# A three-part fused block on one core: the level copies of the gated recurrence go to ScalarE, the state-space scan runs in pairs of steps, and the output's second half is transposed after the first chunk

## The reference

```python
# first block: modulation vectors from a conditioning vector, 6 * D wide for each of two layers
m = jax.nn.silu(cond) @ w_mod + b_mod
# hybrid mixer, gated delta rule in chunks: a unit lower triangular system per chunk and head
lower = where(strict, einsum("nbhcd,nbhsd->nbhcs", kb, kc) * decay, 0)
sol = triangular_solve(lower + eye, rhs, left_side=True, lower=True, unit_diagonal=True)
def step(state, xs_i):                       # 4 steps in each of two directions, in this kernel
    v_new = u_i - einsum("bhcd,bhde->bhce", w_i, state)
    new_state = state * exp(gl_i) + einsum("bhcd,bhce->bhde", kt_i, v_new)
    o_i = einsum(qd_i, state) + einsum(a_i, v_new)
y_lat = concatenate([delta_readout(o_lat_a, za_l, n_tok), o_lat_b], -1) @ w_out   # o_lat_b: softmax attention

# second block: state-space mixer, 32 groups of 16 channels with 64 complex states each
bu = einsum('gph,blgh->blgp', b_bar, uf)     # complex
states = associative_scan(a_bar * s + bu)    # over the 256 tokens
y = einsum('ghp,blgp->blgh', c_re, real(states)) - einsum(..., c_im, imag(states)) + d_skip * uf
y = gelu(y); y = y * sigmoid(einsum('blgh,ghk->blgk', y, w_glu))
```

## Time and profile before

| | us |
|---|---|
| median of 3 runs | 1442.45 |
| the profiled execution | 1443.34 |
| its span | 1441.4 |
| PE busy | 1338.2 (93%) |
| DVE busy | 859.3 (60%) |
| ACT busy | 480.6 (33%) |

### The profile page before, as it was taken

The page is one execution under the profiler, slowest core; times in us unless marked ns, Lnnn a source line. Parts: engine busy times, 40 slices in busy tenths (PEclk is TensorE's granted clock), DMA queues, the critical chain, the costliest instruction groups (busy, mean ns, idle before and its releaser), DMA issues.

```text
span 1441.4 us, 18815 instructions
## 1 busy us (share of the span) xinstructions
PE 1338.2 (93%) x7086; PEld 1000.3 (69%) x7086; DVE 859.3 (60%) x1542; ACT 480.6 (33%) x822; POOL 121.9 (8%) x169
## 2 busy tenths in 40 slices
PE   3899968986899999899999999799999999899997
PEld 1564645553488888687488888677777787588886
DVE  1106795443477767496777677378862242577776
ACT  2243235310343343302553443311213230444443
POOL 0041020000000000200000000244530000000000
PEclk9899978998999999899999999999999999999999
DMA  9221244786745553141445555123233233355541
GB/s 393 78 88 45 100 157 176 286 328 233 275 155 182 201 184 133 67 159 44 150 164 202 184 180 196 64 101 131 93 127 110 109 118 106 130 202 178 196 179 59
DMA packets 24655, 225.69 MB, mean 157 GB/s; under 512 B 2705, under 2 KB 2833, under 8 KB 4370
## 3 DMA queue, kind: packets, MB, share of 16 engines
q1 hardware_dynamic: 23040, 220.31, 41.7%
q10 hardware_dynamic: 1554, 4.56, 0.9%
HBM read 223.81 MB, written 1.05 MB: 156 GB/s over the span
## 4 chain that ended last, share of the span: by engine, by line
PE 84%; DVE 7%; DMA 4%; ACT 3%; issue 1%; ACTq 0%; DVEq 0%
PE psum L751 19%; PE psum L829 15%; PE psum L869 14%; PE psum L830 8%; PE psum L782 6%; PE psum L1382 3%; PE psum L914 3%; DMA ring<-in_w_mod 2%; PE psum L734 2%; DMA h<-in_x 2%; PE psum L942 2%; DVE arena L2119 1%; PE psum L1279 1%; PE psum L705 1%; PE psum L1293 1%
## 5 line engine op out<-in xcount | busy, mean ns | idle before, releaser
L829 PE MATMUL psum<-aT_r,arena_r 128*128 128x512 f32 x920 | 327.5, 398 | 0.5 <-DVE arena_r L2020 0.5
L2020 DVE TENSOR_TENSOR arena_r<-ring,arena_r 128x1024 fp32r<-128x1024 f32 x196 | 229.6, 1221 | 129.0 <-ACT arena_r L1489 129.0
L751 PE MATMUL psum<-aT,ring 128*128 128x256 f32 (+1 forms) x1216 | 303.7, 407 | 1.8 <-DVE aT L1983 1.8
L751 PEld LDWEIGHTS psum<-aT,ring 128*128 128x128 f32 x1216 | 229.1, 191 | 70.0 <-issue 42.4
L830 PE MATMUL psum<-aT_r,arena_r 128*128 128x256 f32 x920 | 258.2, 281 | 0.0
L1489 ACT ACTIVATE arena_r<-ring 128x1024 fp32r<-128x1024 f32 x196 | 194.7, 1050 | 161.3 <-PE psum L869 139.1
L869 PE MATMUL psum<-arena_r 128*128 128x512 f32 x912 | 221.9, 392 | 0.0
L829 PEld LDWEIGHTS psum<-aT_r,arena_r 128*128 128x128 f32 x920 | 172.8, 188 | 42.6 <-issue 0.7
L869 PEld LDWEIGHTS psum<-arena_r 128*128 128x128 f32 x912 | 165.9, 188 | 36.4 <-issue 0.3
L830 PEld LDWEIGHTS psum<-aT_r,arena_r 128*128 128x128 f32 x920 | 173.7, 189 | 2.7
L1501 ACT ACTIVATE nrm<-nrm 128x256 f32<-128x256 f32 x76 | 31.8, 418 | 171.1 <-DVE nrm L2034 171.1
(11 more groups left out here) (428 smaller groups left out, 1545.3 us busy)
## 6 DMA issues: line engine op xcount, KB each, us to landing
ring<-in_w_ffn SPq DMA_DIRECT2D x44, 1536.0 KB, 6.6
ring<-in_w_mod SPq DMA_DIRECT2D x32, 1536.0 KB, 7.4
ring<-in_w_ff SPq DMA_DIRECT2D x32, 1024.0 KB, 4.8
ring<-in_w_in_g SPq DMA_DIRECT2D x8, 1536.0 KB, 6.6
ring<-in_w_conf_i SPq DMA_DIRECT2D x8, 1024.0 KB, 4.7
ring<-in_w_hyb_f SPq DMA_DIRECT2D x4, 1536.0 KB, 6.6
ring<-in_w_in_a SPq DMA_DIRECT2D x4, 1536.0 KB, 6.3
ring<-in_w_in_b SPq DMA_DIRECT2D x4, 1536.0 KB, 6.7
```

The costliest lines, as they stand in the source:

```text
L751: last = mm(bank(use)[:, out_at:out_at + rhs(k).shape[1]], weights[:, k * P:(k + 1) * P], rhs(k), start=(k == 0), stop=(k == KT - 1))
L829: mm(bank(use).rearrange("p (a t) -> p a t", a=2), hi, x_both[:, :, k, :], start=(k == 0), stop=False)
L2020: tt(w_lo[j % 2][:, at], slot(c)[:, at], w_hi[j % 2][:, at].bitcast(F32), ALU.subtract).then_inc(split_ready, 1)
```

## The change

- **Level part.** All engines do the levels sooner. DVE signals after each of its two transposes. ACT takes both copies of `p5`, both of `p6` and all of `q6`, and half of the diagonal copies that POOL made alone. The attention units at these places are taken out: two units stand before `p5`, and the next is in the scan. PE transposes the values behind `p6`, and the first scan step multiplies them directly, where before DVE first copied them into `r_st`.
- **Scan.** `GAPS` becomes strings that give the order of A and M. The query transposes, their second transposes and the key-query products move behind the `vn` products of step 0, those of step 1, and the `ds` products of step 1; DVE's products with the decays go with them.
- **Output product.** `middle` runs after the first chunk.
- **State-space part.** `s5_in` and `s5_out` do two steps at a time, their products alternating between the two steps. Their inputs get four banks instead of two; the projections two instead of four. `s_ri` holds four steps. Some small work (`cum_k`, `glu`, `forget`) moves by a step, and one projection block moves ahead of the second attention.

```diff
@@ PSUM uses
+        if (_s, _what) == (0, "vn"):
+            USE["to_tok"] += beside(2) + _v[2:] + _v[:2]
+        elif (_s, _what) == (1, "vn"):
+            USE["to_feat"] += beside(2)
+        elif (_s, _what) == (1, "ds"):
+            USE["kq"] = beside(2)
...
-USE["in_g"] = BANKS.turn(24)
-USE["s5_u"] = BANKS.turn(S5T, (4, 5))
+USE["in_g"] = BANKS.turn(24, (0, 1))
+USE["s5_u"] = BANKS.turn(S5T, (2, 3, 4, 5))
...
-FORGET = {7: 0, 9: 1, 11: 2, 13: 3, 14: 4, 15: 5}
+FORGET = {7: 0, 9: 1, 11: 2, 14: 3, 15: 4}
 GAPS = {
-    "qk": (2, 1), "p5": (1, 1), "q5": (1, 1), "p6": (1, 1), "q6": (1, 2),
-    "vn0": (2, 2), "ds0": (2, 2), "ks1": (2, 2), "vn1": (2, 2), "ds1": (2, 2),
-    "ks2": (1, 2), "vn2": (1, 2), "ds2": (1, 2), "ks3": (1, 2), "vn3": (0, 3),
+    "qk": "MAMA", "p5": "M", "q5": "M", "p6": "M", "q6": "M", "vn0": "AMM", "ds0": "AMAM", "ks1": "AMA", "vn1": "AMAM",
+    "ds1": "MAMAM", "ks2": "AMAM", "vn2": "MAMAM", "ds2": "AMAM", "ks3": "AMAM", "vn3": "MAMAM",
 }
@@ TensorE
-                    if middle and c == 1:
+                    if middle and c == 0:
...
-                    pe.wait_ge(resid_ready, 2 * s + d + 1)
+                    if s:
+                        pe.wait_ge(resid_ready, 2 * (s - 1) + d + 1)
+                    else:
+                        wait_read(pe, USE["to_tok"][6 + st])
...
+                if s < 2:
+                    (q_tokens, q_features)[s]()
...
+            def s5_in(p):
+                pair = (2 * p, 2 * p + 1)
+                for i in pair:
+                    wait_free(pe, USE["s5_u"][i])
                 for part in range(2):
-                    last = mm(bank(use)[:, part * T:(part + 1) * T], bT[r0:r0 + 32, part, blk, :],
-                              uT[r0:r0 + 32, blk, :], start=True, stop=True)
+                    for i in pair:
+                        use, r0, blk = USE["s5_u"][i], 32 * (i % 4), i // 4
+                        last = mm(bank(use)[:, part * T:(part + 1) * T], bT[r0:r0 + 32, part, blk, :],
+                                  uT[r0:r0 + 32, blk, :], start=True, stop=True)
...
-                if i + 1 < S5T:
-                    s5_in(i + 1)
+                if i % 2 == 0 and i + 2 < S5T:
+                    s5_in(i // 2 + 1)
...
-                if i:
-                    s5_out(i - 1)
+                if i >= 3 and i % 2:
+                    s5_out(i // 2 - 1)
@@ ScalarE
+            act.wait_ge(blocks_inverse, 1)
+            unit_diagonals(1)
+            x, xt = inverse_of(0)
+            for b in range(4):
+                last = fn(XT_m[rows_of_block(b), 0:16, rows_of_block(b)], xt[rows_of_block(b)], ACT.Copy)
+            last.then_inc(xt_copied_first, 1)
+            level_rows(0)
+            level_rows(1)
...
+            for half, use in enumerate(USE["p6"]):
+                wait_full(act, use)
+                freed(fn(blk_p2[:, 8 * half:8 * half + 8, :].rearrange("p a b -> p (a b)"), bank(use), ACT.Copy), use)
...
+            for name in ("qk", "p5", "q5", "p6", "q6"):
+                pause(name)
+            conv_silu(6, (8, 9, 10, 11))
@@ VectorE
             conv5((6, 7))
-            pause("qk")
-
-            use = USE["p5"][1]
-            wait_full(dve, use)
-            freed(v.tensor_copy(blk_p[:, 16:32, :].rearrange("p a b -> p (a b)"), bank(use)), use)
-            conv5((8, 9, 10, 11))
-            pause("p5")
+            next(units)
             use = USE["q5"][1]
```

258 lines of the change are left out of this document (127 added, 131 removed).

## The result

The changed kernel takes 1426.3 us (median of 4 runs, 1422.7 to 1427.7), the kernel before 1441.2 beside it: ratio 0.9896, 95% interval 0.9878 to 0.9914. It is faster by 15, and I had forecast 36.8 (1405.6, with a range of 1394 to 1421). A second set of runs gave 1426.3 again (0.9894, interval 0.9867 to 0.9921). The profiled execution took 1426.4, its span is 1424.6.

The account below looks back on a forecast made before the run. PE was taken to bound nearly everything. Gains of 23 (level part and scan), 0.8 (output product) and 13 (state-space part) summed to 36.8: 1443.3 to 1406.5 profiled, 1405.6 in runs, range 1394 to 1421.

Parts of the forecast that it names:

- The two counts are nearly equal: Scan's end: 329.2 by PE's count, 327.6 by the chunks' at 5.24 us each; 3 added for disturbance gave 332.
- PE's own count: Scan: 106.7 us of PE work plus 3.5 of new waiting, from the first scan product at 219.0 to 329.2.
- The term of 23: Level part and scan together: scan ends at 332 against 354.9, a gain of 23 us, ends 8 and 28.
- The level part: Middle stage before the scan: a shorter chain lets the scan begin at 219.0, 27.7 us earlier.
- the halving: State-space input and output products: two steps in turn overlap and halve their 32.6 us, saving 16.3.
- The 13: State-space part: 16.3 saved less 1.5 and 1.9 of waiting, 12.9, taken as 13 us, ends 0 and 16.
- The output product: Middle stage after the scan: `middle` behind the first chunk covers PE's 0.84 wait for ACT's copy, gain 0.8 us.
- the scan that gives its gain back: Rival, chance 0.18: PE waits in the scan for DVE's work as in the level part; gain 8, result 1420.6.
- Chunks came hardly faster: Rival "The chunks come faster", chance 0.08: evenly freed slots leave only PE's count in the scan; 1402.9, or 1399.6.
- Pairs did overlap: Rival "The pairs do not overlap", chance 0.12: the state-space part gains nothing but some waiting of DVE; 1418.6.
- no projection block waited for ScalarE in two banks: Rival "It ends slower", chance 0.04: with two projection banks, ACT's waits in the state-space part cost PE 45 us; 1450.6.
- The waits forecast at 3.5 and 1.9: 3.5 us: scan's query transposes wait for ACT; 1.9: PE waits for DVE's short convolution at the state-space part's end.

Follow-up runs that it names:

- short chunks: Only the first 192 of 3072 columns of each w_mod chunk loaded from the seventh on, output not the reference's: changed kernel 1410.2 us, kernel before 1424.5.
- e6: Changed kernel with one modulation product more in the pauses of the second scan step, one less in the last pause: 1425.9 us, ratio 0.9909.
- e12: Changed kernel with state-space small work moved, read-out transposes behind the second chunk, and two modulation products moved early into the second scan step: 1418.0 us, ratio 0.9826.
- e8: Changed kernel with pairs kept, but both parts of one step written first, then both of the other, not in turn: 1426.0 us.
- e17: Changed kernel with state-space small work moved and the read-out's transposes behind the second chunk of the output product again: 1415.4 us, ratio 0.9822.
- e5: Changed kernel with state-space small work moved: forget(3), forget(4) behind steps 13, 14, cum_k(2) behind the last output pair, skip(3) ahead of forget(5): 1423.6 us, ratio 0.9865.

## Why the prediction was wrong

- *The step that failed* is the scan's "The two counts are nearly equal, so each will disturb the other; I take 3 for that". PE's own count came out (110.2, measured 110.5 with short chunks), in part by luck, as the windows show. But the 3 for the disturbance measured 11 in the scan of the profiled run (6 to 13 over seven traces), and the level part, for which I had none, paid 6 more: together as much as the transfers cost before. I set a count of chunks "asked without pause" beside PE's and took the larger. The chunks are not asked without pause, since a slot is freed only by a product that stands in PE's order: no transfer ran from 229.1 to 234.8 and from 252.8 to 262.8. That each such delay is paid where it occurs is my reading; closing the second gap (e6, e12) did not shorten the scan reliably. The term of 23 measured 12.8. Its upper end of 28 is also 1.2 too low by my own sum (354.9 - 219.0 - 106.7 = 29.2).
- *The level part*: 27.7 forecast, 25.3 measured, and 30 with short chunks. Nothing in my sum stood for the pauses in `q5`; the kernel before has one of 0.5. The 6.4 was half hidden in the total by the clock, which stayed high in `p5` and its product, and by a quicker relay.
- *The state-space part*: the halving held, but the alternation of neighbours, from which I argued it, was not needed (e8). The 13 became 5.3 for one sub-term, 1.5 taken for 8.25: `forget(3)` behind step 14 means that PE waits for a whole step of 7.4, as VectorE does not pause there. Of 7.7 missing, 5.4 came back by moving it.
- *The output product*: 0.8 forecast, -3.4 measured. I looked at who needs the transposes, and not at what queues behind them: the second chunk's slot, and the feed-forward weights that wait for it.
- *The rivals*: the nearest in price is the scan that gives its gain back (1420.6), but for another reason: VectorE and ScalarE held PE up there for 6.0, of which 3.2 was foreseen and 1.8 stands just ahead of the output product, where the kernel before waits 1.0. Chunks came hardly faster: 5.07 each, where I had 5.24, is 310 GB/s. The Trainium skill (DMA: Bandwidth & Descriptors, opening table) gives some 358 GB/s for a core. The stage from 260 to 343 averaged 292, under it; single slices of 0.65 us reach 473, so the figure bounds no short stretch here. Pairs did overlap, and no projection block waited for ScalarE in two banks.
- The waits forecast at 3.5 and 1.9 measured 3.2 and 1.8.

## What to carry to other kernels

Where a stream of weights and an engine are both nearly full, removing idle time elsewhere does not remove the waits for the stream: price the stage once with the transfers shortened, in both kernels, and compare runs by their ratio to a kernel that ran beside them. When a piece is moved ahead of a product that frees a buffer, look for the load behind that buffer, and for the work behind the load. When small work is hung behind a loop step of a busy engine, its waiter pays up to a whole step; move both ends, or the wait only moves on.

## What the runs showed of the hardware

- Packets of 16 KB of a queue of instructions took 0.9 to 1.7 us in this stage, and PE's pauses in `q5` ended 2.2 to 2.9 behind the start of one, in 28 of 28. Two such starts beside chunks: 205.89 in the changed kernel, when most of the chunk was through, and 202.94 in e17, in the hole between two. One pause cost up to 6.4 (e5). I had not expected either that the run with the lower clock in `p5` would have the shorter level part.
- The transfers cost PE more than its waits for them: in the scan of the kernel before, PE's busy time was 93.6 at a mean clock of 0.94 with whole chunks, and 89.0 at 0.98 with short ones.
- Two products on different rows or output rows of the array ran together whether they were written in turn or one step after the other (e8): eight instructions take 1.06 to 1.14, where four took 1.06, some 2.0 times the rate. The Trainium skill (TensorE: Matmul & The Clock Gate, on packing small matmuls) has 3.07 for four; here two give 2.0, and the row of the convolution 4.6 for four.
- With short chunks the runs of a kernel spread over 1.3 to 3.1 us (four kernels, four runs each), with whole ones over 3.2 to 12.9 (four to ten runs each): much of the variation between runs goes with the transfers.
